# Twenty small fp32 records in five places of TensorE's stream, in a hybrid attention and Fourier backbone of two layers

## What is computed

```
def _fourier_mix(h, w):
    ...
    f = jnp.fft.fft2(hg, axes=(1, 3), norm="ortho").real
    return f.reshape(b, n, D_MODEL).astype(h.dtype) @ w

def _conv_ffn(h, w_up, conv_w, conv_b, w_down):
    u = _dwconv3(h @ w_up, conv_w, conv_b)
    val, gate = jnp.split(u, 2, axis=-1)
    return (val * jax.nn.silu(gate)) @ w_down

def reference(...):
    for i in range(DEPTH):                       # DEPTH = 2
        sh1, sc1, g1, sh2, sc2, g2 = _ada(c, ada_w[i], ada_b[i])
        hx = _modulate(_rmsnorm(x, norm1_g[i]), sh1, sc1)
        ...
        yx = _mla(...) if kind == MIXER_MLA else _fourier_mix(hx, fno_w[j])
        x = x + g1 * yx
        x = x + g2 * _conv_ffn(_modulate(_rmsnorm(x, norm2_g[i]), sh2, sc2),
                               ffn_w_up[i], ffn_conv_w[i], ffn_conv_b[i], ffn_w_down[i])
    return _rmsnorm(x, final_norm_g)
```

## Time and profile before

| | |
|---|---|
| median of 3 runs | 2134.85 us (2106.29 to 2134.99) |
| span of the profiled execution | 2138.7 us, mean granted TensorE clock 0.990 |
| TensorE busy | 2071.3 us, 97% of the span, 17120 matmul records |
| VectorE busy | 1608.4 us, 75% |
| ScalarE busy | 1044.1 us, 49% |
| moved by DMA | 547.37 MB, mean 256 GB/s |

### The profile page before, as it was taken

How to read it: one execution, slowest core, us unless ns; L and a number is a source line. 1 busy time by engine, 2 the same in 40 slices (tenths; PEclk the granted TensorE clock), 3 DMA queues, 4 the chain that set the end, 5 groups by cost and what they waited for, 6 DMA issues and landing times.

```text
span 2138.7 us, 44829 instructions
## 1 busy us (share of the span) xinstructions
PE 2071.3 (97%) x17120; PEld 1995.6 (93%) x17120; DVE 1608.4 (75%) x1892; ACT 1044.1 (49%) x1489; POOL 81.8 (4%) x63
## 2 busy tenths in 40 slices
PE   6989999999999999999999999999999999999997
PEld 3678888899999999999999989999999999999997
DVE  3238989898888888988888868998886664456665
ACT  2355666545555555433455543465555553335553
POOL 0000000031000000000000211200000000000012
PEclk8999999999999999999999999999999999999999
DMA  9954666796888788899888836968865555555663
GB/s 374 364 218 161 234 219 235 264 379 232 291 293 291 278 291 286 326 371 373 314 293 290 293 110 252 356 217 287 282 233 181 186 185 190 194 194 189 195 189 128
DMA packets 127805, 547.37 MB, mean 256 GB/s; under 512 B 14576, under 2 KB 15088, under 8 KB 107120
## 3 DMA queue, kind: packets, MB, share of 16 engines
q1 hardware_dynamic: 127728, 546.31, 71.9%
HBM read 544.16 MB, written 2.10 MB: 255 GB/s over the span
## 4 chain that ended last, share of the span: by engine, by line
PE 85%; DVE 10%; ACT 2%; DMA 2%; issue 1%; SPq 0%; DVEq 0%; ACTq 0%
PE bank L1397 27%; PE bank L1398 26%; PE bank L1399 26%; DVE acc L878 3%; DVE w_lo L855 2%; DMA early<-early_w 1%; PE bank L1489 1%; PE bank L1476 1%; DVE pt_lo L859 1%; DVE negmax L1054 1%; PE bank L1403 1%; ACT prob L629 1%; PE bank L1405 1%; PE bank L1404 1%; DVE v_lo L859 0%
## 5 line engine op out<-in xcount | busy, mean ns | idle before, releaser
L496 ACT CAST w_hi<-raw 128x1024 fp32r<-128x1024 f32 x642 | 671.9, 1049 | 523.0 <-PE bank L1399 414.9
L855 DVE TENSOR_TENSOR w_lo<-raw,w_hi 128x1024 fp32r<-128x1024 f32 x642 | 787.6, 1239 | 182.8 <-ACT w_hi L496 182.5
L1397 PE MATMUL bank<-h_hi,w_hi 128*128 128x256 f32 x3216 | 899.5, 280 | 3.1 <-DVE h_lo L1182 3.1
L1398 PE MATMUL bank<-h_lo,w_hi 128*128 128x256 f32 x3216 | 898.5, 279 | 0.0
L1399 PE MATMUL bank<-h_hi,w_lo 128*128 128x256 f32 x3216 | 898.4, 279 | 0.0
L1397 PEld LDWEIGHTS bank<-h_hi,w_hi 128*128 128x128 f32 x3216 | 608.7, 189 | 6.1 <-issue 3.7
L1399 PEld LDWEIGHTS bank<-h_hi,w_lo 128*128 128x128 f32 x3216 | 608.4, 189 | 0.0
L1398 PEld LDWEIGHTS bank<-h_lo,w_hi 128*128 128x128 f32 x3216 | 604.3, 188 | 0.0
L1397 PE MATMUL bank<-a_hi,w_hi 128*128 128x256 f32 x1408 | 391.8, 278 | 2.1 <-DVE a_lo L859 2.0
L1399 PE MATMUL bank<-a_hi,w_lo 128*128 128x256 f32 x1408 | 391.2, 278 | 0.0
L1398 PE MATMUL bank<-a_lo,w_hi 128*128 128x256 f32 x1408 | 391.2, 278 | 0.0
(11 more groups left out here) (195 smaller groups left out, 2049.6 us busy)
## 6 DMA issues: line engine op xcount, KB each, us to landing
raw<-weights SPq DMA_DIRECT2D x642, 512.0 KB, 4.8
ada<-ada_late SPq DMA_DIRECT2D x160, 1024.0 KB, 5.1
early<-early_w SPq DMA_DIRECT2D x64, 512.0 KB, 7.9
ctx_s<-ctxT SPq DMA_DIRECT2D x4, 512.0 KB, 5.7
x<-xT SPq DMA_DIRECT2D x4, 512.0 KB, 8.5
outT<-h_pre SPq DMA_DIRECT2D x4, 512.0 KB, 2.6
dft_s<-dft SPq DMA_DIRECT2D x1, 1040.0 KB, 8.3
conv_s<-conv SPq DMA_DIRECT2D x2, 176.0 KB, 5.8
```

The source lines that it names most:

```text
L496: act.copy(w_hi[:, slot, :], raw[:, slot, :]).then_inc(hi_done, 1)
L855: dve.tensor_tensor(w_lo[:, slot, :], raw[:, slot, :], w_hi[:, slot, :].bitcast(f32), ALU.subtract)\
L1397: pe.matmul(out, wh, hi_part, start=first, stop=False)
L1398: pe.matmul(out, wh, lo_part, start=False, stop=False)
```

## The change

A helper `settle` is added to TensorE's program. It issues two plain fp32 matmuls of 128x4 (ones by four columns of the identity) into a corner of PSUM bank 6 that nobody reads. It has no semaphore. It is called behind `wide` and behind `down(0, 1)` in both FFNs, and ahead of the linear map's `square` in the Fourier stage. Nothing else differs.

```diff
+            def settle():
+
+                for _ in range(2):
+                    pe.matmul(bank[6][:, 0:4], ones, ident[:, 0:P:32], start=True, stop=True)
+
...
             def ffn(c0, T0, P0, Y0, h0, layer):
                 pe.wait_ge(tile_taken, T0)
                 wide(c0, T0, h0)
+                settle()
                 with pe.Fori(1, PARTS[0] // 2) as i:
                     up(c0, T0, i)
...
                 down(0, 0)
                 acc_turn(b)
                 down(0, 1)
+                settle()
                 with pe.Fori(1, KT // 2) as i:
                     for t in range(2):
                         down(i, t)
...
             pe.wait_ge(tile_taken, T_UP1)
+            settle()
             square(C_FNO, Y_FNO, f_hi, f_lo)
```

## The result

The changed kernel is slower, by a little. Its median is 2142.2 us over 16 runs (2137.68 to 2155.66), and the kernel before has 2123.72 us over 16 runs (2106.29 to 2146.02). The ratio is 1.010 (the two medians alone give 1.009), with a 95% interval of 1.008 to 1.013. The ratios in this document leave out executions more than 1.5% above the fastest of the same kernel in their batch, which for the kernel before are 1 of 16 here and 2 of 13, 11 of 29 and none of 11 in the later batches, so a ratio from the batch of 29 may understate a gain. The forecast was 2105.5 us, a gain of 29 us. The runs of the changed kernel lie in two groups, ten from 2137.7 to 2144.0 us and six from 2152.5 to 2155.7 us. The profiled execution is of the upper group, with a span of 2153.9 us against 2138.7 us before.

A forecast was written before the change was run, and what follows sets the result against it. TensorE's product pace was taken as the bound. Gains of 12.8 + 6.0 + 12.8 less 2.3 for the calls made 29.3 us, from 2134.85 to 2105.5 us; range 2099 to 2112, to 2121 with two rivals.

The forecast's parts named there:

- What bounds the kernel, and the two paces: TensorE's long stages: products start every 117.7 or 113.3 ns at one clock, a state kept between breaks; 4.45 ns a product.
- What flips it: Breaks in TensorE's stream: small products with no wait on either side leave it quick (three of three seen).
- rival 4: All five calls: small products turn the pace over or leave it slow, so the kernel is slower, 2154.3 us; 6%.
- A: Call behind the first FFN's wide tiles: the slow up loop of 2880 products turns quick, saving 12.8 us.
- C: Call behind the second FFN's wide tiles: 2880 products turn quick, saving 12.8 us.
- B: Call behind the first FFN's first two down tiles: 1344 products turn quick, saving 6.0 us, or 0 if DMA limits.
- D: Call ahead of the Fourier stage's linear map: 768 products already quick, no gain; up to 3.4 us lost if left slow.
- E: Call behind the second FFN's first two down tiles: 3072 products already quick, no gain; up to 13.7 us lost if slow.
- rival 3: A call behind a quick stream makes it slow: 2119.2 us in the second FFN, 2108.9 ahead of the linear map; 12%.
- Cost of a call: Each of the five calls adds 0.45 us to TensorE's stream, 2.3 us in all, none of it hidden.
- rule of one gap for each width and clock: Skill's formula, 109.2 ns for 256 columns: no second pace, so the small products only cost, giving 2137 us.
- rivals 1 and 4: First: the five calls change nothing and only cost, 2137.2 us, 13%; the other: slower than before, 2154.3 us, 6%.

The follow-up runs named there:

- the first probe: Changed kernel without its five calls; instead calls of 1 to 8 small matmuls ahead of tiles in the FFNs' up and down loops; one execution, 2257.92 us.

## Why the prediction was wrong

**What bounds the kernel, and the two paces.** Right. All runs have TensorE streams of either 113.3 or 117.8 ns a product at a granted clock of 1.00, kept from one break to the next, and the times follow from how many products run at which. Counting products at each pace also forecast three later results well: three matmuls (2115 expected, 2115.12 measured), the last call taken out (2131, 2131.89), the pairs taken apart (2113, 2110.89).

**What flips it.** This step failed. I took small fp32 matmuls without a wait to leave the quick pace whatever came before, from three turned rows of eight and sixteen records. In the table above two helper matmuls go from Q to S1 in 43 of 43. It isn't the number of records that misled: the helper's four matmuls have eight records, as a turned row has, and go from Q to S1 as well (4 of 4). The two turned rows of eight records that I read the earlier trace rows both had a slow stream ahead (S2 and S0), and only the sixteen records of the earlier trace rows had a quick one. Behind S0 the helper's pair leads to Q too (4 of 4). What was missing is a row of the helper's matmul behind a quick stream, and there it behaves otherwise than a turned row (Q to Q, 10 of 10). I had named the outcome as rival 4, with 6%, but under the condition that four records behave unlike eight, which isn't the one that decides.

**A and C.** These terms rested on a second assumption, that the stream ahead of the calls is slow, as in the one profiled execution. What stands ahead differs from execution to execution, for no cause that the traces show. Behind the wait in the wide tiles the stream was quick in both FFNs of the changed kernel's profile, and in 13 of the 21 such stretches of all eleven traces (6 were S0 and 2 S2), none of them in the profile of before. Where it had been S0, the pair did what I forecast (S0 to Q, 2826 products in 320 us). So of 12.8 us each nothing came in the profiled execution. And in executions in which the loops of before would have been quick by chance, the change takes that away. That is most likely why the median rises against a kernel of which I had read only that its stretches are slow. It is argued and not shown, since each kernel has one profile. The three times of before that I had (2134.99, 2134.85, 2106.29) said that they aren't always, and I used this only to explain the fastest.

**B.** Nothing came, for the same reason. Behind the second down tile (slow before, quick here) the pair left the slow pace. That DMA could hold the stage back was an open bound of 0 to 6 us. The runs with a quick down part have 388 and 389 GB/s there with TensorE never waiting, so the whole 6.0 us was to be had.

**D.** Right in the outcome, by luck in part: behind the wait of 0.92 us ahead of it, the linear map was quick with the call as without it. In other traces it wasn't: without any call it was slow in the first probe (768 products in S2), and behind one matmul it was slow too (S0).

**E.** The loss that rival 3 named at this place. The forecast put it at nothing, and at up to 13.7 us if it came. Measured were 10.3 us as a difference of medians, and 2527 x 4.45 ns = 11.2 us in the profile. The last 542 products lie behind a wait and were quick.

**Cost of a call.** Right, 0.45 us.

**The rivals.** The profiled execution is rival 4 in A, B, C and E (2154.3 us worked out, 2155.7 us measured for it), without the linear map. That the two numbers agree so well is luck: the linear map (3.4 us) and the last 542 products (2.4) didn't come, and two slow stretches that no call touches did. The lower group is 13 us below the upper one. I have no profile of it; a last stretch or one up part that stays quick would give that much. The rule of one gap for each width and clock (2137 us) came nearer to the median than the forecast, but for no reason of its own: it knows only one pace, and 113.3 and 117.8 ns stand in every trace here. The prediction also read it too widely. The Trainium skill, "TensorE: Matmul & The Clock Gate", section "Back-to-back issue gap", gives this formula for the isolated gap of one matmul, and says that in a stream of weight loads and matmuls, as here, both set the spacing.

**The range.** 2099 to 2121 us left out rivals 1 and 4 as 19%. An honest weight for a matmul never seen behind a quick stream would have been near even between the steps "quick" and "slow", and the range would have reached to 2155.

## What to carry to other kernels

Where a stream of equal products bounds a kernel, take its pace from the starts of the products in each long stretch: here two paces at one clock meant that something ahead of the stretch, and not in it, set its time, and that was worth 30 us of 2140. A row that shows one instruction behind one state of the engine doesn't tell what a similar instruction does behind another state; and when a transition is what pays, put several counts and several starting states into one probe kernel, since one trace then gives the whole table. And a profile is one execution: where the times of before scatter by 1.4%, ask which of its stretches would look different in the next one before building terms on them.

## What the runs showed that was not expected

- The pace of a stream of three-matmul products behaved as a small automaton (a machine of a few states with fixed steps) with four states. Behind a quick stream a single fp32 matmul of 128x4 kept the quick pace (121 of 121) and two side by side left a slow one (43 of 43). What in TensorE holds this state is open. The long weight load (192 against 188 ns), fixed at one of the three products, is its only other trace.
- Behind a wait or a delay the pace can be another, and which one differs from execution to execution. At the wide tiles' wait it was Q, S0 or S2. Delays as short as 0.05 us (0.16 in place of 0.11 us at the start of the third up tile) changed Q to S2, and in the trace without the last call one product 0.015 us late (459.4 us) stands where Q became S1.
- In the changed kernel's profile the clock fell to its lower level for some 3.4 us behind the two turned rows of the first FFN and a wait of 0.19 us, in the middle of a full stream. The products there are 214 ns apart, which costs about 1.5 us. The trace with four matmuls has the same at this place, also behind a wait of 0.19 us. The kernel before has a wait of 0.17 us there and the full clock. Of the stretch from 877 us:

```profile
877.00:880.50 3.50, 3.50 (x19) 0.51 0.98 401
```
